# Loads of the C tables in GpSimd's queue, a second buffer for backward states, gate tiles moved, first loads reordered, some matrices loaded earlier

## What is computed

```python
def _s5_direction(u_ctx, u_lat, lam, dt, bmat, cmat):     # for 2 directions, 128 groups of 16 channels, 64 states
    lam_bar = jnp.exp(lam * dt[:, None])
    b_bar = ((lam_bar - 1.0) / lam)[..., None] * bmat
    # h[t] = lam_bar * h[t-1] + b_bar u[t],  y[t] = Re(cmat h[t]); context first, its last state starts the latent part
...
    y_l = d_skip * ul + sum over both directions (the second on flipped sequences)
    y = gelu(y); ya, yb = split(y @ w_glu + b_glu); out = ((ya * sigmoid(yb)) * silu(g)) @ w_out
```

## Time and profile before

| | before |
|---|---|
| median of 3 runs | 1804.78 us |
| profiled execution, its own time | 1805.32 us |
| its span | 1803.5 us, 23250 instructions |
| TensorE busy | 1613.9 us (89%) |
| VectorE busy | 730.6 us (41%) |
| ScalarE busy | 366.5 us (20%) |
| GpSimd busy | 0.2 us |
| DMA moved | 264.25 MB, mean 147 GB/s |
| chain that ended last | PE 79%, DVE 6%, DMA 5%, SPq 5%, ACT 3%, issue 2% |

### The profile page before, as it was taken

How to read it: one execution, slowest core, us unless ns; L and a number is a source line. 1 busy time by engine, 2 the same in 40 slices (tenths; PEclk the granted TensorE clock), 3 DMA queues, 4 the chain that set the end, 5 groups by cost and what they waited for, 6 DMA issues and landing times.

```text
span 1803.5 us, 23250 instructions
## 1 busy us (share of the span) xinstructions
PE 1613.9 (89%) x9548; PEld 1055.0 (58%) x9548; DVE 730.6 (41%) x1543; ACT 366.5 (20%) x850; POOL 0.2 (0%) x4
## 2 busy tenths in 40 slices
PE   2899969989988969999866999999799999899999
PEld 1454535646644545675565888884345554488853
DVE  3888834435469894355526001101310122132310
ACT  0222233223211121322122100000112442121200
POOL 0000000000000000000000000000000000000000
PEclk8899989989989979999988999999899999899999
DMA  9544550200575563566668233444333213344441
GB/s 236 212 159 158 204 215 1 97 32 1 176 222 195 169 242 70 188 191 200 161 196 236 96 141 140 167 159 163 126 140 140 94 47 112 121 140 140 151 163 60
DMA packets 213322, 264.25 MB, mean 147 GB/s; under 512 B 49023, under 2 KB 134369, under 8 KB 212961
## 3 DMA queue, kind: packets, MB, share of 16 engines
q1 hardware_dynamic: 167664, 217.99, 37.4%
q10 hardware_dynamic: 45553, 44.76, 7.3%
HBM read 226.16 MB, written 36.57 MB: 146 GB/s over the span
## 4 chain that ended last, share of the span: by engine, by line
PE 79%; DVE 6%; DMA 5%; SPq 5%; ACT 3%; issue 2%; ACTq 0%; DVEq 0%
PE bank L427 75%; PE bank L430 4%; SPq L2287 2%; DMA memory<-mc_scratch 2%; DMA mc_scratch<-memory 1%; SPq L2324 1%; SPq L2265 1%; SPq L2274 1%; DMA memory<-in_s_c_im 1%; DMA k_scratch<-memory 0%; DMA memory<-in_w_mod 0%; ACT memory L1150 0%; DVE memory L1797 0%; DVE memory L1808 0%; DVE memory L1806 0%
## 5 line engine op out<-in xcount | busy, mean ns | idle before, releaser
L427 PE MATMUL bank<-memory 128*32 128x128 f32 (+8 forms) x8784 | 1519.3, 374 | 84.2 <-DMA memory<-mc_scratch 17.8
L427 PEld LDWEIGHTS bank<-memory 128*128 128x128 f32 (+3 forms) x8784 | 961.7, 164 | 597.3 <-issue 467.2
L430 PE MATMUL bank<-memory 128*128 128x128 f32 (+1 forms) x764 | 113.5, 295 | 101.5 <-DVE memory L2157 16.8
L430 PEld LDWEIGHTS bank<-memory 128*128 128x128 f32 (+1 forms) x764 | 94.9, 151 | 146.6 <-issue 84.5
L2240 DVE SCALAR_TENSOR_TENSOR memory<-bank,memory 128x255 f32<-128x255 f32 x44 | 21.0, 478 | 113.3 <-ACT memory L1552 113.3
L2084 DVE TENSOR_TENSOR memory<-memory 128x256 f32<-128x256 f32 x56 | 23.3, 416 | 102.7 <-ACT memory L1368 102.7
L1191 ACT ACTIVATE memory<-bank 128x512 f32<-128x512 f32 x64 | 34.9, 595 | 105.3 <-PE bank L430 105.1
L2133 DVE TENSOR_SCALAR memory<-bank,memory 128x256 f32<-128x256 f32 x16 | 6.6, 478 | 120.6 <-PE bank L427 120.6
L1929 DVE TENSOR_REDUCE memory<-bank 128x1 f32<-128x512 f32 (+1 forms) x48 | 30.2, 684 | 60.3 <-PE bank L427 60.3
L1275 ACT ACTIVATE memory<-bank,memory 128x512 f32<-128x512 f32 (+1 forms) x64 | 36.3, 579 | 85.5 <-DVE memory L1932 85.5
L1452 ACT ACTIVATE memory<-bank,memory 128x256 f32<-128x256 f32 x16 | 6.3, 474 | 214.4 <-PE bank L427 214.4
(11 more groups left out here) (235 smaller groups left out, 889.9 us busy)
## 6 DMA issues: line engine op xcount, KB each, us to landing
memory<-in_s_w_glu SPq DMA_DIRECT2D x16, 2048.0 KB, 8.9
memory<-in_w_mod SPq DMA_DIRECT2D x12, 2048.0 KB, 12.0
memory<-in_w_ffn_up SPq DMA_DIRECT2D x22, 1024.0 KB, 6.9
memory<-in_w_in SPq DMA_DIRECT2D x10, 2048.0 KB, 7.6
mb_scratch<-memory ACTq DMA_DIRECT2D x32, 512.0 KB, 2.7
mc_scratch<-memory ACTq DMA_DIRECT2D x32, 512.0 KB, 4.0
memory<-mb_scratch SPq DMA_DIRECT2D x32, 512.0 KB, 5.4
memory<-mc_scratch SPq DMA_DIRECT2D x32, 512.0 KB, 6.5
```

Of the source, the lines that this page charges most:

```text
L427: return nc.tensor.matmul(o, l, r, start=start, stop=stop, skip_group_check=free)
L430: return nc.tensor.transpose(o, i, ident[0:n, 0:n])
```

## The change

- `poles_load` and `mc_load` move from SP to a new program for GpSimd. It issues the 12 pole loads at once, then waits for the last stores of the matrices and k tables, and then loads all 32 mc matrices in order, each behind the output unit that frees its buffer (the same waits as before).
- Opening, SP: the fourth modulation load and the head weights stand ahead of `b_load(0)` and `c_load(0)`; `b_load(1)` goes behind gate load 1. TensorE: the transposes of the pole tables go behind head tile 0, those of C behind head tile 2, in banks 0 to 3. VectorE: 8 steps of the poles instead of all that are left ahead of the fourth modulation row, the rest behind `modulated`. ScalarE: the copies of C stand before head tile 3's squares.
- `b_load(2)` writes to hT's last quarter (`bbar_(2)`) and stands behind the second load of query weights; `c_load(2)` stands behind the wait for `v_mm` of head 7; the second out0 load goes ahead of the last key product's wait.
- `xs_back`: two buffers for the backward states; recurrence(q) waits for the outputs of q - 2.
- TensorE and ScalarE: gate tiles 24 to 27 leave additions 8 to 15; all of 24 to 31 stand among additions 24 to 31 and outputs 16 to 23, and direct(2, 1) and direct(3, 0) stand further forward. The ring order of the S5 weights changes to fit.
- `small` shrinks from 256 to 248 columns, and the places that signal through it move.

```diff
-S5IN_ORDER = (4, "u0", 5, "u1", 6, "u2", "u3", 7)
+S5IN_ORDER = (4, "u0", 5, "u1", "u2", "u3", 6, 7)
...
+        def bbar_(q):
+            return hT_flat[:, 3072:4096] if q == 2 else bbar[:, q % 2, :]
...
+        xs_back = (xs_rev, take(NCL * 32))
...
                 last.then_inc(*S.up("head_mm", t))
+                if t == 0:
+                    pe.wait_ge(*S.at("lam_ready"))
+                    b = bank(pe, ("lamT",), [("lamT",)], 0)
...
+                if t == 2:
+                    for ql in range(2):
+                        c_turned(0, ql, 2 + ql)
...
-            additions(8, 11)
-            gate_tile(24)
-            additions(11, 13)
-            gate_tile(25)
-            additions(13, 15)
-            gate_tile(26)
-            additions(15, 16)
-            gate_tile(27)
+            additions(8, 16)
...
             additions(24, 27)
+            gate_tile(24)
+            additions(27, 30)
+            direct(2, 1)
+            gate_tile(25)
+            additions(30, 32)
+            gate_tile(26)
+            outputs(16, 19)
+            gate_tile(27)
+            outputs(19, 21)
+            direct(3, 0)
             gate_tile(28)
-            additions(27, 30)
+            outputs(21, 23)
             gate_tile(29)
-            additions(30, 32)
-            direct(2, 1)
-            outputs(16, 19)
+            outputs(23, 24)
             gate_tile(30)
-            outputs(19, 22)
             gate_tile(31)
-            outputs(22, 24)
             y_turned(0)
             y_turned(1)
-            direct(3, 0)
             direct(3, 1)
...
             mod_row(0, 2)
             mod_columns(0, 1)
-            advance(100)
+            advance(8)
             mod_row(0, 3)
             mod_columns(0, 2)
             mod_columns(0, 3)
             for c in range(2):
                 modulated(0, c)
+            advance(100)
...
-                    if b == 0 and q:
-                        dve.wait_ge(*S.at("yc_mm", 8 * q - 1))
+                    if b == 0 and q >= 2:
+                        dve.wait_ge(*S.at("yc_mm", 8 * q - 9))
...
+        @block.gpsimd
+        def _(pool):
...
+            poles_load()
...
+            for u in (29, 30, 31):
+                pool.wait_ge(*S.at("mc_out%d" % (u % 3), u))
+            for kp in (14, 15):
+                pool.wait_ge(*S.at("k_out%d" % (kp % 2), kp))
+            mc_load(0, NU)
...
-            for ct in range(3):
+            for ct in range(4):
                 ring(("mod", 0, ct))
-            poles_load()
+            ring("head_in")
             b_load(0)
             c_load(0)
-            b_load(1)
-            ring(("mod", 0, 3))
-            ring("head_in")
             for ct in range(4):
                 ring(("gate", ct))
                 if ct == 1:
+                    b_load(1)
                     c_load(1)
...
             ring(("uq", 1))
-            for ct in range(2, 6):
+            b_load(2)
+            for ct in range(2, 4):
+                ring(("mod", 1, ct))
+            sp.wait_ge(*S.at("v_mm", 7))
+            c_load(2)
+            for ct in range(4, 6):
                 ring(("mod", 1, ct))
             ring(("out0", 0, 0))
+            ring(("out0", 0, 1))
             sp.wait_ge(*S.at("k_mm", H - 1))
-            b_load(2)
-            c_load(2)
             b_load(3)
-            ring(("out0", 0, 1))
+            ring(("out0", 1, 0))
             c_load(3)
-            ring(("out0", 1, 0))
             ring(("out0", 1, 1))
```

More of the change, by code:

```diff
@@ L155, in take @@
                 n = int(np.prod(shape))
[L156 removed]
+                assert at[0] + n <= 53208, (at[0] + n, shape)
                 v = sb[:, at[0]:at[0] + n]
@@ L173, in build @@
         bmod = take(DEPTH * 6, P)
-        small = take(256)
+        small = take(248)
         ring_at = at[0]
@@ L516, in _ @@
                 x_transposes(0, c)
-            pe.wait_ge(*S.at("lam_ready"))
-            b = bank(pe, ("lamT",), [("lamT",)])
-            for i in range(4):
-                last = tr(b[:, i * P:(i + 1) * P], sc_a[:, 10 + i, :])
-            last.then_inc(*S.up("lamT_mm"))
-            pe.wait_ge(*S.at("drow"))
-            b = bank(pe, ("dT",), [("dtab",)])
-            tr(b[:, 0:NU // 2], drow, NU // 2).then_inc(*S.up("dT_mm"))
-            for ql in range(2):
-                c_turned(0, ql, None)
             w = weights(pe, "head_in", (KD, HEAD_IN))
@@ L535, in _ @@
                 last.then_inc(*S.up("head_mm", t))
+                if t == 0:
+                    pe.wait_ge(*S.at("lam_ready"))
+                    b = bank(pe, ("lamT",), [("lamT",)], 0)
+                    for i in range(4):
+                        last = tr(b[:, i * P:(i + 1) * P], sc_a[:, 10 + i, :])
+                    last.then_inc(*S.up("lamT_mm"))
+                    pe.wait_ge(*S.at("drow"))
+                    b = bank(pe, ("dT",), [("dtab",)], 1)
+                    tr(b[:, 0:NU // 2], drow, NU // 2).then_inc(*S.up("dT_mm"))
+                if t == 2:
+                    for ql in range(2):
+                        c_turned(0, ql, 2 + ql)
             for n in range(16):
@@ L804, in outputs @@
                                     if dr:
-                                        st = over(xs_rev[r, ri * 16 + n:ri * 16 + n + 1], (32, NCL))
+                                        st = over(xs_back[q % 2][r, ri * 16 + n:ri * 16 + n + 1], (32, NCL))
                                     else:
@@ L1203, in unit_stored @@
                     act.dma_start(k_dram[kp], kt[:, kp % 2, :]).then_inc(*S.up("k_out%d" % (kp % 2), kp, by=16))
-            for ql in range(2):
-                c_conjugated(0, ql)
             for t in range(NTT):
+                if t == 3:
+                    for ql in range(2):
+                        c_conjugated(0, ql)
                 act.wait_ge(*S.at("head_mm", t))
@@ L1405, in _ @@
             by_channel(1)
-            additions(8, 11)
-            gates_in(24, 25)
-            additions(11, 13)
-            gates_in(25, 26)
-            additions(13, 15)
-            gates_in(26, 27)
-            additions(15, 16)
-            gates_in(27, 28)
+            additions(8, 16)
             by_token(2, 0, 2)
@@ L1768, in _ @@
             link(V.memset(bbd.rearrange("p a n -> p (a n)"), 0.0))
-            V.tensor_copy(small[0:1, 251:252], small[0:1, 200:201]).then_inc(*S.up("bbd_zero", 0))
+            V.tensor_copy(small[0:1, 241:242], small[0:1, 200:201]).then_inc(*S.up("bbd_zero", 0))
             def b_scaled(q):
@@ L1950, in values @@
                 dve.wait_ge(*S.at("pt2", h))
-                V.tensor_copy(small[0:1, 250:251], small[0:1, 200:201]).then_inc(*S.up("pt", (h, 2)))
+                V.tensor_copy(small[0:1, 240:241], small[0:1, 200:201]).then_inc(*S.up("pt", (h, 2)))
             def gated(h):
@@ L2017, in _ @@
             link(V.memset(bbd.rearrange("p a n -> p (a n)"), 0.0))
-            V.tensor_copy(small[0:1, 251:252], small[0:1, 200:201]).then_inc(*S.up("bbd_zero", 1))
+            V.tensor_copy(small[0:1, 241:242], small[0:1, 200:201]).then_inc(*S.up("bbd_zero", 1))
             for u in range(16, 24):
@@ L2065, in _ @@
             link(V.tensor_copy(over(powN[:, 32:33], (256, 8), (64, NB), (1, 32)), im))
-            V.tensor_copy(small[0:1, 251:252], small[0:1, 200:201]).then_inc(*S.up("lam_tables"))
+            V.tensor_copy(small[0:1, 241:242], small[0:1, 200:201]).then_inc(*S.up("lam_tables"))
             def recurrence(q):
@@ L2103, in recurrence @@
                     link(tt(o, row(ctx, c), row(scan, 64), ALU.add))
-                V.tensor_copy(small[0:1, 252:253], small[0:1, 200:201]).then_inc(*S.up("ctx_done", q))
+                V.tensor_copy(small[0:1, 242:243], small[0:1, 200:201]).then_inc(*S.up("ctx_done", q))
                 for b in range(4):
@@ L2152, in rms @@
                     if i == 0:
-                        V.tensor_copy(small[0:1, 252 + t:253 + t], small[0:1, 200:201]).then_inc(*S.up("x_rms", (i, t)))
+                        V.tensor_copy(small[0:1, 242 + t:243 + t], small[0:1, 200:201]).then_inc(*S.up("x_rms", (i, t)))
                 for t in range(2):
@@ L2229, in _ @@
             for t in range(2):
-                V.tensor_copy(small[0:1, 252 + t:253 + t], small[0:1, 200:201]).then_inc(*S.up("x_rms", (1, t)))
+                V.tensor_copy(small[0:1, 242 + t:243 + t], small[0:1, 200:201]).then_inc(*S.up("x_rms", (1, t)))
             rms(1)
@@ L2369, in _ @@
             mb_load(0, 3)
[L2370 removed]
             t_load(0, 0)
             ring(("s5u", 1))
[L2373 removed]
+            ring(("s5u", 2))
             mb_load(3, 8)
[L2375 removed]
+            ring(("s5u", 3))
             mb_load(8, 11)
             t_load(0, 1)
[L2378 to L2381 removed]
+            mb_load(11, 19)
+            ring(("s5in", 6))
+            t_load(1, 0)
             ring(("s5in", 7))
[L2383 to L2386 removed]
             t_load(1, 1)
```

73 lines of the change are left out of this document (29 added, 44 removed).

## The result

| | before | after |
|---|---|---|
| median | 1805.53 us (4 runs) | 1781.88 us (4 runs, 1776.51 to 1784.75) |
| ratio | | 0.9859 [0.9835, 0.9883] |
| profiled execution, span | 1805.32, 1803.5 us | 1776.51, 1774.7 us |
| TensorE busy, mean granted clock | 1613.9 us, 0.952 | 1608.3 us, 0.961 |

What follows compares the result with a forecast made beforehand. TensorE, busy 1613.9 of 1803.5 us, bounds the kernel, so only its some 190 us of waiting can be won. Gains of 16.4 + 8.5 + 28 = 52.9 us off 1805.3 give 1752.4, range 1742 to 1777.

Steps and rivals of the forecast that it cites:

- Opening: 0 to 62 us: poles by GpSimd and an earlier fourth modulation load start the head sooner; gain 16.4 us, 6 to 20.7.
- floor by data: Opening: 10.5 MB at 401 GB/s are in by some 29 us, product 3.64 us, so no head before about 39.5.
- VectorE then needs 14.25 us to the third modulation row: Opening: time from poles in to third row, read from before's trace (30.44 to 44.69), kept for the earlier start.
- Between attention and S5 matrices: 490 to 507 us: loading B and C for unit 2 earlier removes TensorE's wait; gain 8.5 us, 6.8 to 9.
- S5 stage: 726 to 1000 us: matrices by GpSimd, second xs_rev and new order cut TensorE's waits; gain 28 us, 15 to 34.
- replay: S5 stage: new order stepped through from 726 with unit costs; last turn at 963.5 instead of 997.4, 33.9 us sooner.
- L: S5 stage: time from the output unit freeing a buffer until GpSimd's next matrix is there; 6.7 us taken, bounds 5 and 14.4.
- (c): S5 stage: slow GpSimd matrices hold up every group of three outputs, making the kernel slower, up to 1817 us; chance 0.04.
- The rule weighed: Skill's rule that more issuing engines save only sequencer time, leaving the S5 stage little gain; prediction held order, not bandwidth, limiting.
- (a): Opening and S5 stage: GpSimd's issues take several us each, so gain is 30 us, time 1775; chance 0.13.
- (b): Transfers were the limit, engines full: opening gives 10, S5 stage 20, in all 38 us, time 1767; chance 0.13.
- (d): The opening gains nothing, since head weights or poles come late; time 1769; chance 0.06.

Runs made afterwards that it cites:

- e2_bmod512: d1_after512 with the four b_mod loads ahead of x, ctx and s_d in ScalarE's queue: 45.9 us faster than before (0.9754).
- d1_after512: Changed kernel with `small` packed into 128 columns, all behind it 512 bytes lower than in before: 33.8 us faster than before (0.9812).
- f1_half_tables: d1_after512 with four of eight DMAs left out of each S5 table but the first (output wrong): 47.4 us faster than before (0.9735).
- e1_tables_pool: d1_after512 with the S5 stage's table loads issued by GpSimd instead of SP: 39.9 us faster than before (0.9782).

## Why the prediction was off

**What bounds the kernel, and where.** Right: 27.4 us came from the three stretches named, 1.5 us came just behind them, and then the two traces run in parallel at 28.9 us distance.

**Opening: 16.4 forecast, 12.3 at the head, 8.4 kept.** The poles were in by 15.4, earlier than the low bound of 16. The floor by data (39.5) lies close to the 40.6 of e2_bmod512, but by luck: the fourth block was in at 32.8 and not at 29, and its product took 1.96 us at the full clock and not 3.64. The step that failed is "VectorE then needs 14.25 us to the third modulation row". That interval was taken from a trace in which b_mod had long landed, since VectorE was itself kept until 30.44; moved forward 15 us, the rows came to stand before their second operand, and waited 8.43 us: 22.6 us from the start of the chain to the third row. A second term was too small for a reason of its own: 5.6 us from the fourth row to the head were 7.9, with the clock at 0.69 there, against 0.98 between 54.8 and 61.7 in before. The two, 8.4 us at the third row and 2.3 behind the fourth, less 0.4 between these rows, are the whole distance from the 39.2 that the step gives with the poles in at 15.4 to the head at 49.45. Shown by e2_bmod512: with b_mod early the head comes 8.0 us sooner than in d1_after512 (40.62 against 48.59), 5.4 of it up to the fourth row and 2.6 between that row and the head. The 1.5 us for the transposes inside the head were 1.7. The other 2.2 us were lost between head and attention: 1.6 at TensorE's wait near 144 (4.04 us against 3.31) and in the slower tile behind it, most of the rest near 227. The pole tables, costed at nothing, lie there; that they caused it isn't shown.

**Between attention and S5 matrices: 8.5 forecast, 9.6 to 10.7 measured** (18.0 less 8.4 at the first out0 tile, 19.2 at the second, 18.5 at 726). Right in mechanism and size. VectorE took the scaling of B at 488.65 and unit 16 at 492.42, as the step has it.

**S5 stage: 28 forecast, 8.9 measured, 19.6 with the good layout.** Two terms failed.
- The layout. "The second xs_rev is a new address in the same instructions and costs nothing" was the only word on addresses, and of the 8 columns taken from `small` to make room for it there was none. In before's order a shift of 128 bytes, with nothing else, costs 22.2 us; in the new order the 32 bytes cost 10.1 (d1_after512 against the changed kernel), and this stage alone is 10.8 longer for them. Why the cost is lower there isn't shown; fewer waits of the new order end on a transfer, which would fit. It is also what made parts of the change look like losses: with the good layout the opening alone gains 9.1 us and the S5 edits 15.5. The early matrices alone were not run with it.
- Crowding. Of the replay's 33.9 us I gave back 6 for clock and crowding; with the good layout 14.3 would have been right. The replay itself is sound up to the first additions: it has 4.4 and 3.3 us idle there, and d1_after512 shows 4.91 and 2.15. Set to the same start it is then 3.5 us early at direct(0,1), 6.3 at direct(2,0), 12.7 at direct(3,0) and 14.2 at the last turn; it falls behind most between direct(2,0) and direct(3,0), where two tables and the matrices are in flight together. It gave each load the landing of a quiet moment (5.55 in the chain) whatever else was moving; f1_half_tables shows that 9.2 us of this stage hang on half of the tables' transfers. L, from issue to landing, was 7.4 by the median (the issue is in it) and 10 at the first output matrix (issued 793.22, used from 803.3), where 6.7 was taken; by the sum's own price of 4 us per us, 7.4 costs 3 us. The sum is also not at one with itself: it puts the stage's gain at 15 us for L = 11, where the prices of rival (c), 4 us per us up to 9.1 and 8 beyond, leave 3 of the 28. With these the low end of the range would have been near 1789, and the measured time inside it.

**The rule weighed.** I said that the trace disagrees with the Trainium skill, DMA: Bandwidth & Descriptors, section Issuing engines are not separate DMA queues, since the engines had moved 2 GB/s between 830 and 842. That window was misread: TensorE was busy for 12.00 of its 12 us, so no matrix was missed in it, and where TensorE did stand 10.3 us for a matrix, between 900 and 913.3, the engines moved 266 GB/s. Order did count as well: with the matrices in a queue of GpSimd's own, and the other edits of this stage, the waits on mc_scratch went from 17.8 to 8.1. But for the tables the runs agree with the rule: moved to another issuer, they cost the same (e1_tables_pool), and halved, they cost 9 us less (f1_half_tables).

**Rivals and chances.** (a) is ruled out: GpSimd issued a load of the poles or of a matrix in 0.51 to 0.58 us. (b) was true of the tables and matrices and had 0.13; its time, 1767, is near what the change gives with the good layout (1772), by another split than its 10 and 20. (c) did not come as a whole, but in part: the median of L stayed under its 9.1, while 11 of the 32 matrices took longer (12.0 at most). (d) is ruled out by the head at 49.45. No case had the layout, and the range (1742 to 1777) was left by 5 us; with the layout undone the changed kernel, at 1772, lies inside.

**What would show it.** Right: no wait on C, mc_scratch below 10, a new wait near the additions 11 to 14 (9.9 us for 8, listed under "issue" and not under mb_scratch), the 15.5 us wait for xs_rev gone. Half right: units earlier, by 15.3 us for the first three and 19 from the fourth, not 24. Wrong: head at 49.5 (40 to 47), k_scratch 2.7 (none).

## What to carry to other kernels

When work is moved forward, go through every operand of its first instructions, not only those whose wait the trace shows: what had long landed where the work stood may be late where it goes. A size cut in an allocator is an edit to every address behind it; keep DMA sources and targets at the alignment they had (multiples of 512 bytes here) or time that edit by itself, above all before judging parts of a change one by one. And where loads meet, cost them by what is in flight together, not by the landing of a lone one; a queue of its own repairs order, not bandwidth.

## What the runs showed of the hardware

- Moving all tensors behind one by 32 or 128 bytes of the partition, from starts at multiples of 512, cost 24.7 and 22.2 us of 1806 with the same instructions; the same packets took 5.5% and 4.3% more engine time. Shifts of 64 and 128 bytes cost 2 to 7 us less than 32, with the same edits. A multiple of 256 bytes was not timed.
- GpSimd issued DMAs of 128 partitions and 512 KB in 0.54 us each, and eight table DMAs in 4.5 us where SP needed 4 to 12, standing in its own busy queue. Landings were hardly slower for it: 6.6 us (median) for the matrices in the S5 stage of d1_after512 (between 720 and 990), where SP's in before took 6.4.
